# Reordering the opening of a hybrid convolution and sparse-attention layer: input rows first, small rotation angles, modulation in three parts, three projection tiles by channel tile

## What is computed

```python
mod = jax.nn.silu(c) @ w_ada + b_ada
shift, scale, gate = jnp.split(mod, 3, axis=-1)
h = rmsnorm(x, norm_in) * (1.0 + scale[:, None, :]) + shift[:, None, :]
proj = h @ w_in
(cb, cc, cu, cz, aq, ak, av, az, iq, ik, iw) = jnp.split(proj, cuts, axis=-1)
...
q = rope_partial(aq.reshape(Bsz, L, N_HEADS, HEAD_DIM), positions)
k = rope_partial(ak.reshape(Bsz, L, N_HEADS, HEAD_DIM), positions)
q_idx = rope_partial(iq.reshape(Bsz, L, N_IDX_HEADS, IDX_DIM), positions)
k_idx = rope_partial(ik[:, :, None, :], positions)[:, :, 0, :]
```

## Time and profile before

| | before |
|---|---|
| median of 3 runs | 732.51 us (732.18 to 734.01) |
| profiled execution, of which span | 737.07 us, 735.3 us |
| PE busy | 669.7 us, 91% of the span |
| PE weight loads busy | 552.7 us, 75% |
| DVE, ACT, POOL busy | 492.1, 364.9, 235.4 us |
| chain that ended last, by engine | PE 79%, DVE 8%, ACT 5%, issue 5%, DMA 2% |
| mean granted TensorE clock | 0.981 |

### The profile page before, as it was taken

How to read it: one execution, slowest core, us unless ns; L and a number is a source line. 1 busy time by engine, 2 the same in 40 slices (tenths; PEclk the granted TensorE clock), 3 DMA queues, 4 the chain that set the end, 5 groups by cost and what they waited for, 6 DMA issues and landing times.

```text
span 735.3 us, 8771 instructions
## 1 busy us (share of the span) xinstructions
PE 669.7 (91%) x3170; PEld 552.7 (75%) x3170; DVE 492.1 (67%) x737; ACT 364.9 (50%) x550; POOL 235.4 (32%) x113
## 2 busy tenths in 40 slices
PE   0489999899999999999999989998999988979996
PEld 0478988678888888888888877886777666758885
DVE  4786815677888899998079550014898988485734
ACT  1484435555563143452444434535787787783212
POOL 0003324432224152757766488420011110030000
PEclk9999999999999999999999999998999999989998
DMA  8902287353222110111100462075744340301531
GB/s 343 412 26 86 63 212 141 114 171 113 90 86 87 57 56 32 57 36 50 58 29 29 137 196 69 1 171 163 239 115 116 87 115 9 107 29 58 172 115 57
DMA packets 22661, 79.14 MB, mean 108 GB/s; under 512 B 3738, under 2 KB 4058, under 8 KB 21596
## 3 DMA queue, kind: packets, MB, share of 16 engines
q1 hardware_dynamic: 22620, 78.60, 35.2%
HBM read 61.77 MB, written 13.41 MB: 102 GB/s over the span
## 4 chain that ended last, share of the span: by engine, by line
PE 79%; DVE 8%; ACT 5%; issue 5%; DMA 2%; SPq 0%; ACTq 0%; DVEq 0%
PE ps L631 17%; PE ps L632 17%; PE ps L633 17%; PE ps L810 4%; PE ps L812 4%; PE ps L811 4%; PE ps L748 3%; DMA wa<-in_w_ada 2%; PE ps L689 2%; PE ps L690 2%; PE ps L670 2%; PE ps L671 2%; DVE phL L1384 2%; DVE acc L1178 1%; PE ps L761 1%
## 5 line engine op out<-in xcount | busy, mean ns | idle before, releaser
L631 PE MATMUL ps<-hH,wH 128*128 128x512 f32 (+1 forms) x592 | 230.3, 389 | 3.8 <-ACT wH L865 2.3
L632 PE MATMUL ps<-hL,wH 128*128 128x512 f32 (+1 forms) x592 | 228.3, 386 | 0.0
L633 PE MATMUL ps<-hH,wL 128*128 128x512 f32 (+1 forms) x592 | 228.1, 385 | 0.0
L1533 POOL TENSOR_TENSOR wL<-raw,wH 128x1024 fp32r<-128x1024 f32 x37 | 94.4, 2552 | 186.5 <-ACT wH L865 186.5
L631 PEld LDWEIGHTS ps<-hH,wH 128*128 128x128 f32 x592 | 111.9, 189 | 25.1 <-issue 3.0
L633 PEld LDWEIGHTS ps<-hH,wL 128*128 128x128 f32 x592 | 111.9, 189 | 21.5
L632 PEld LDWEIGHTS ps<-hL,wH 128*128 128x128 f32 x592 | 112.1, 189 | 19.2
L1376 DVE CUSTOM_DVE_ANT_0 ps<-ps,bias 128x128 f32<-128x128 f32 (+3 forms) x64 | 48.7, 761 | 45.6 <-PE ps L671 43.7
L1384 DVE TENSOR_TENSOR phL<-ps,phH 128x512 fp32r<-128x512 f32 (+1 forms) x96 | 52.7, 555 | 22.6 <-ACT phH L1040 18.5
L1020 ACT ACTIVATE relu<-ps,wabs 128x384 f32<-128x384 f32 (+5 forms) x48 | 40.1, 849 | 43.6 <-PE ps L690 17.5
L1270 DVE SCALAR_TENSOR_TENSOR score<-relu,wsgn,score 128x384 f32<-128x384 f32 (+5 forms) x42 | 49.7, 1183 | 17.2 <-ACT relu L1020 14.5
(11 more groups left out here) (206 smaller groups left out, 1102.9 us busy)
## 6 DMA issues: line engine op xcount, KB each, us to landing
raw<-in_w_units SPq DMA_DIRECT2D x36, 512.0 KB, 3.3
wa<-in_w_ada SPq DMA_DIRECT2D x8, 1024.0 KB, 8.8
ks<-qk_halves SPq DMA_DIRECT2D x32, 256.0 KB, 5.5
xin<-in_x SPq DMA_DIRECT2D x8, 512.0 KB, 12.5
gw<-in_w_ada SPq DMA_DIRECT2D x8, 512.0 KB, 4.4
qs<-qk_halves SPq DMA_DIRECT2D x16, 256.0 KB, 4.0
wo<-in_w_out SPq DMA_DIRECT2D x8, 512.0 KB, 9.3
xe<-in_x SPq DMA_DIRECT2D x8, 512.0 KB, 4.1
```

The costliest lines, as they stand in the source:

```text
L631: pe.matmul(out, wH[:, n % 2, kt, :], hH[:, kt, cols], start=(kt == 0), stop=False)
L632: pe.matmul(out, wH[:, n % 2, kt, :], hL[:, kt, cols], start=False, stop=False)
L633: mm = pe.matmul(out, wL[:, n % 2, kt, :], hH[:, kt, cols], start=False, stop=(kt == KT - 1))
L1533: g.tensor_tensor(wL[:, n % 2, :, :], raw[:, n % NRAW, :, :], wH[:, n % 2, :, :].bitcast(F32), ALU.subtract).then_inc(s_wL, 1)
```

## The change

- **Order of loads.** The positions (as 8 rows of 128), `w_ik` and x come first, `w_ada` after them.
- **Angles.** DVE works on 128x64 angles, 8 frequencies by 8 token tiles: PE transposes the positions, eight products make the angles, ACT takes sine and cosine, DVE widens each to 128x1024 (`wide`), PE transposes them in 16 tiles, and ACT copies them to `tabS` and `tabC`.
- **Modulation in parts.** The columns of `w_ada` are summed for channel tiles 0 to 3, 4 and 5, 6 and 7 (`PARTS`), each with its own `acc`, products and `shift` and `amp`. The first part is 8 DMAs of 512 KB in rows of 2 KB, the others 8 DMAs of 256 KB each in rows of 1 KB. The second part's buffers lie on those of the first, so SP waits for the first sum (`s_acc` of 8) before it issues them.
- **x.** The transposed channel tiles 2 to 7 are copied to `xT` by ACT without scale and shift (`STAGED`), and 0 and 1 stay in PSUM. ACT does all eight scalings and all eight roundings; DVE's three are gone.
- **Three units by channel tile.** Units 0, 1 and 2 run interleaved (`FIRST_STEPS`), with the products of modulation parts 2 and 3 among them. The weights have 4 slots at first; DVE makes `wL` of units 1 and 2. The transposes of `iw` move behind unit 3.

```diff
-NRAW = 2
+NFIRST = 3
+NSLOT = 4
-        ("iq", 0): [("iwt", 0)],
+        ("iq", 2): [("iwt", 0)],
-X_GROUPS = ((0, 4), (4, 6), (6, 7), (7, 8))
+X_GROUPS = ((0, 4), (4, 6), (6, 8))
+PARTS = ((0, 4), (4, 6), (6, 8))
+STAGED = (2, 3, 4, 5, 6, 7)
+X_TURNS = ((2, 2, 0), (3, 4, 0), (4, 6, 0), (5, 0, 0), (6, 2, 1), (1, 4, 2), (7, 6, 3), (0, 0, 4))
+FIRST_STEPS = ([(0, 0), (0, 1), (1, 0), (1, 1), (0, 2), (1, 2), (2, 0), (2, 1), (2, 2), (3, 0), "mod", (3, 1), (3, 2)]
+               + [(4, 0), (4, 1), (4, 2), (5, 0), "mod", (5, 1), (5, 2)]
+               + [(6, 0), (6, 1), (7, 0), (7, 1), (6, 2), (7, 2)])
...
+            sp.dma_start(posi[:], a["positions"].rearrange("o (b p) -> (o b) p", p=P)).then_inc(s_pos, 16)
+            load(0)
             for t in range(NB):
                 sp.dma_start(xin[:, t, :], a["x"][0, P * t:P * t + P, :]).then_inc(s_x[t], 16)
+            def load_part(g):
+                lo_k, hi_k = PARTS[g]
+                each = KT // len(wa[g])
+                for i, dst in enumerate(wa[g]):
+                    if g == 1 and i == 0:
+                        sp.wait_ge(s_acc, KT)
+                    for k in range(each):
+                        sp.dma_start(dst[:, k, :, :], w_cols[:, each * i + k, :, P * lo_k:P * hi_k]).then_inc(s_wa[g][i], 16)
+            load_part(0)
             load(1)
+            load(2)
+            load_part(1)
+            load_part(2)
+            load(3)
+            sp.dma_start(pairs[:], a["pairs"]).then_inc(s_pairs, 16)
+            for n in range(NSLOT, NSLOT + 2):
+                load(n)
...
+            pe.wait_ge(s_tab, 1)
+            modulation(0, 2)
+            pe.wait_ge(s_tab, 2)
+            part = 1
+            for at_step in FIRST_STEPS:
+                if at_step == "mod":
+                    if part > 1:
+                        pe.wait_ge(s_amp, part)
+                    modulation(part, 7)
+                    part += 1
+                else:
+                    first_unit(*at_step)
```

More of the change, by code:

```diff
@@ L433, in wait_low, with raw_count, wait_wl @@
                 waits.wait_ge(s_splP, m + 1 - NT)
[L435 to L438 removed]
+        def raw_count(n):
+            return 1 if n < NSLOT else (n - NSLOT) // 2 + 2
+        def wait_wl(waits, n):
+            if n in (1, 2):
+                waits.wait_ge(s_wLd, n)
             else:
[L440 removed]
+                waits.wait_ge(s_wL, max(1, n - 1))
         block = ctx.enter_context(nc.Block())
@@ new lines, in _, with table @@
+            for kt, bank, staged in X_TURNS[4:]:
+                pe.wait_ge(s_xt, staged)
+                for t in range(NB):
+                    mm = turn_x(kt, bank, t)
+                mm.then_inc(s_xtp, 1)
+            def table(src, bank):
+                for b in range(NB):
+                    mm = pe.transpose(two(bank)[:, P * b:P * b + P], src[:, b, :, :].rearrange("p r f -> p (r f)"), identF[:])
+                mm.then_inc(s_tabp, 1)
+            pe.wait_ge(s_wide, 1)
+            pe.wait_ge(s_xt, 5)
@@ new lines, in first_unit @@
+            def first_unit(kt, n):
+                pe.wait_ge(s_hH, kt + 1)
+                w = (S - IQ0) // 2 if UNITS[n][0] == "iq" else HALF
+                if kt == 0:
+                    pe.wait_ge(s_wH, n + 1)
+                for half in range(2):
+                    out = ps[:, 2 * slot(n) + half, 0:w]
+                    cols = slice(S - w * (2 - half), S - w * (1 - half))
+                    pe.matmul(out, wH[slot(n)][:, kt, :], hH[:, kt, cols], start=(kt == 0), stop=False)
+                    if kt == 0 and half == 0:
+                        wait_wl(pe, n)
+                    pe.matmul(out, wL[slot(n)][:, kt, :], hH[:, kt, cols], start=False, stop=False)
+                    if half == 0:
+                        pe.wait_ge(s_hL, kt + 1)
+                    mm = pe.matmul(out, wH[slot(n)][:, kt, :], hL[:, kt, cols], start=False, stop=(kt == KT - 1))
+                if kt == KT - 1:
+                    mm.then_inc(s_unit, 1)
@@ new lines, in _ @@
+            factors(0, 2)
+            first_low(1)
+            ada_sum(1, 0)
+            low_h(0)
+            first_low(2)
+            ada_sum(1, 1)
+            low_h(1)
+            ada_sum(1, 2)
+            low_h(2)
+            ada_sum(1, 3)
+            low_h(3)
+            ada_sum(2, 0)
+            factors(1, 7)
+            ada_sum(2, 1)
+            low_h(4)
+            ada_sum(2, 2)
+            low_h(5)
+            ada_sum(2, 3)
+            factors(2, 7)
+            low_h(6)
```

324 lines of the change are left out of this document (178 added, 146 removed).

## The result

The changed kernel took 728.86 us, the median of 8 runs (725.82 to 730.38), beside 733.06 us (732.18 to 736.91) for 8 runs of the kernel before: a ratio of 0.9932, 95% interval 0.9908 to 0.9956, so about 5.0 us less (3.2 to 6.7). The ratio is that of the means; the medians alone differ by 4.2 us. The forecast was 725.0 us, in a range of 722.5 to 731.0, and faster with a chance of 0.78. Its profiled execution took 727.11 us, where the forecast for a profiled one was 729.6. In the later comparisons one execution of each kernel took far longer (863.57 us before, 964.55 us after, at granted clocks of 0.76 and 0.66), and the ratios leave these out.

A forecast was written before the change was run, and what follows sets the result against it. PE bounds the kernel from 56.5 us, so the opening's saving counts as what it moves unit 5 forward: 98.2 to 90.7, 7.5 us. On the median, 732.5 - 7.5 = 725.0 us, range 722.5 to 731.0.

The forecast's parts named there:

- Loads, angles, normalisation: Opening: squares from 9.4 us, last x group ready at 20.9 and done at 22.5, part 1's sum ending at 32.0.
- The rival of slow rows: `w_ada` loads: rows of 2 and 1 KB stream badly, part 1 takes 24.2 us, total 735.7; chance 0.10.
- The 42 us: Part 1's 16 loads of 256 KB: estimate by the skill's fit if they did not overlap, kernel some 30 us slower.
- the fast pace: PE in the opening: 0.12 us per record, so part 1's products take 1.9 us, to 34.0, factors at 34.7.
- the slow pace: Part 1's products on PE: 0.21 to 0.22 us per record instead of 0.12, which would add 1.5 us.
- The 16 x 0.12: Part 1's one-column products on PE: 16 at 0.12 us each, 1.9 us in all.
- Channel tiles: Units 0 to 2: `hH` 0 at 37.0, `hL` 1 at 42.0, 1.4 us lost at each of tiles 4 and 6.
- The rival that the clock falls in these stalls: Channel tiles 4 and 6: one or two falls of PE's clock, total 726.7 to 728.4 us; chance 0.20.
- Unit 5: DVE chain of 14.0 us, weights at 90.6, PE waits 1 us, start about 90.7 instead of 98.2: 7.5 earlier.
- The step that failed: Behind unit 6's weights: every step hangs on PE's own evacuations as before, and 3.8 us of `relu` waits stay.
- 98 to 110 us, 90% busy for 173 GB/s: Old trace's DMA window, used as the rate for slow `w_ada` rows: part 1 in 24.2 us, to 40.4.
- Its own sign of being wrong: Behind the opening: the forecast is wrong if a later wait grows by what the opening gains.

The follow-up runs named there:

- fillers: Changed kernel plus 14 and 22 transposes that nobody reads, ahead of and behind the products of part 1: 726.69 us, ratio 0.9911 to the kernel before.
- repeats of after: Changed kernel run twice more, unedited: first repeat 728.06 us, ratio 0.9909 to the kernel before; traced executions 728.69 and 726.71 us.
- repeats of before: Kernel before run twice more, unedited, each as one execution: 731.92 and 734.81 us.
- later scores: Changed kernel with the first group of index scores moved from step 4 of its unit to step 8: 725.58 us, ratio 0.9885 to the kernel before.
- all three edits: Changed kernel with filler transposes, index scores after 8 steps, and POOL's third split after DVE turned `ik`: 721.65 us, ratio 0.9834 to the kernel before.
- `w_ada` first: Changed kernel with part 1 of `w_ada` loaded and summed ahead of x: 737.67 us, ratio 1.0046 to the kernel before.
- units one by one: Changed kernel with units 0, 1 and 2 one after the other instead of interleaved: 736.68 us, ratio 1.0042 to the kernel before.
- later split: Changed kernel with POOL's third split waiting until DVE has turned `ik`: 725.88 us, ratio 0.9883 to the kernel before.
- parts together: Changed kernel with all modulation parts summed and multiplied before the first projection product: 741.76 us, ratio 1.0111 to the kernel before.

## Why the prediction held, point by point

**Direction and mechanism were right.** PE's dense row of products bounds the kernel, and what the opening saves counts at unit 5. Undoing the interleaving, the parts or the order of the loads each gives back the whole gain and ends 3 to 8 us behind the kernel before.

**Loads, angles, normalisation.** Squares at 8.22 (forecast 9.4), the last x group normalised at 20.5 (22.5), the sum of part 1 at 31.0 (32.0). The forecast for accumulations was 1.25 each; they took 1.38 (9.63/7), and the earlier start paid for that. The rival of slow rows was wrong: 390 and 354 GB/s, and no wait for `w_ada`. The 42 us worked out from the fit of the Trainium skill (DMA: Bandwidth & Descriptors, Anatomy of one DMA), for 16 loads that do not overlap, did not come. The page gives its fit for DMAs that GpSimd issues, and these are SP's; here SP issued the 16 from 30.98 to 40.04 us and they landed 5.9 us behind their issue in the median, so they did overlap.

**The transposes and products of part 1: half wrong.** The transposes took the fast pace, as forecast, and `tabS` was out at 29.3 instead of 32.1. That opened the hole: the sum ended only at 31.0, PE idled for 2.04 us, and the products took 3.25 instead of 1.9. The step "it has transposed densely since 19 us, so I take the fast pace" looked at the work before the products, not at the gap between. I had priced the slow pace at 1.5; the measured difference is 1.3 (3.25 against 1.93 with fillers), and 0.9 in both repeats (2.86 and 2.85). The 16 x 0.12 counts records; the products are 8. The factors came at 34.8 (34.7) all the same, since all in front was a microsecond early.

**Channel tiles.** `hH` 0 at 37.1 (37.0), `hL` 1 at 42.1 (42.0), 1.2 us lost at each of tiles 4 and 6 (1.4), the products of parts 2 and 3 at 0.95 (1.0), unit 3 at 72.7 (72.2) without a gap. The rival that the clock falls in these stalls was wrong: the windows from 42 to 116 us read 1.00, and the only mark of the stalls is the single products right behind a wait, 0.50 us instead of 0.40.

**Unit 5.** Chain of DVE 14.07 us (14.0), weights ready at 91.24 (90.6), a gap of 1.06 (1), start at 91.34 (90.7). Over three traces each the gain is 6.5 us instead of 7.5: 0.8 of it from the later start in the new kernel (91.5 for 90.7; in the first trace DVE begins `ik` at 72.96 for the 72.3 of the forecast), 0.2 from the old one's mean (98.0 for 98.2).

**The step that failed** is "from there every step hangs on PE's own evacuations as before; the 3.8 us of `relu` waits stay". What stands there is a queue of transfers. SP's last issue of `iqs` and a window of the kernel after:

```profile
105.74 1.87 SPq L540 DMA_DIRECT2D iqs<-hlL  x3
...
110.00:116.00 6.00, 6.00 (x28) 4.95 (x28) 0.00 (x0) 2.55 (x3) 2.54 (x4) 1.00 1.04 205
```

The same two of the kernel before:

```profile
110.16 1.87 SPq L502 DMA_DIRECT2D iqs<-hlL  x3
...
110.00:116.00 6.00, 6.00 (x28) 4.95 (x28) 3.50 (x3) 3.47 (x4) 2.40 (x1) 1.00 1.05 181
```

In both, the DMA engines are busy all the time and move half of what they can (205 and 181 GB/s beside 390 at 20 to 25 us). The last issues end at 107.6 and 112.0, and the piece lands about 12 us behind, at 119.44 in the kernel after. The queue runs empty in the windows of one microsecond that follow, first in the kernel before, then in the kernel after:

```profile
123.00:124.00 1.00, 1.00 (x6) 0.88 (x5) 0.65 (x1) 0.98 (x2) 0.00 (x0) 1.00 0.06 16
```

```profile
119.00:120.00 1.00, 0.56 (x3) 0.59 (x4) 1.00 (x1) 0.00 (x0) 1.00 (x1) 1.00 0.04 16
```

So the transfers came some 4 us earlier. PE, though, reaches the first score at 116.78, before at 123.42, 6.6 earlier, and waits 2.66 us. In the kernel before it came less than 1 us behind the queue's end, and in one repeat it waited 1.4 us for it. The working in the prediction had the seed of it: it put unit 3's evacuation 5.4 us earlier (86.3 for 91.70; it was 4.7) and unit 5's start 7.5, and the stores and loads of the turned units follow the evacuation. I read the earlier trace rows at 98 to 110 us, 90% busy for 173 GB/s, as a price for the loads of `w_ada` and not as the queue that it is.

**Why the step cost next to nothing.** The `relu` waits did not stay, and what they lost is about what the DMA wait gained. The table has each trace from unit 5 to the last index score, in us; PE busy is that of the stretch.

| | stretch | waits of PE, the longest | granted clock, ten us at that wait | PE busy |
|---|---|---|---|---|
| before | 123.8 | 3.8, 3.1 | 0.83 | 120.0 |
| repeats of before | 122.2, 124.9 | 3.6, 1.5 and 3.7, 2.9 | 1.00 and 0.66 | 118.6 and 121.2 |
| after | 123.5 | 3.4, 2.7 | 0.83 | 120.1 |
| repeats of after | 124.3, 124.4 | 4.1, 3.4 and 4.0, 3.3 | 0.83 and 0.83 | 120.2 and 120.3 |
| fillers | 122.6 | 4.1, 3.4 | 1.00 | 118.5 |
| later scores | 121.7 | 3.1, 1.6 | 1.00 | 118.6 |
| all three edits | 122.1 | 3.8, 2.3 | 1.00 | 118.3 |

The waits sum to 3.6 to 3.8 us before and 3.4 to 4.1 after. Moving the scores takes the DMA wait away and brings 3.1 us of `relu` back, which bears the exchange out. That the total came out as forecast is luck, since the prediction had no DMA wait in it and kept all of the other. Its own sign of being wrong, a later wait that grows by what the opening gains, came in part: 2.7 of the 6.5 us.

The rest is the clock. Behind the long wait it falls in both kernels, in two traces of three before and in all three after. The kernel before, then the kernel after:

```profile
130.00:140.00 10.00, 7.80 (x29) 6.62 (x30) 6.29 (x10) 4.56 (x8) 1.25 (x1) 0.83 0.39 129
```

```profile
120.00:130.00 10.00, 10.00 (x41) 8.46 (x40) 7.77 (x7) 3.52 (x7) 4.46 (x2) 0.83 0.37 114
```

PE is busy for 118.3 to 118.6 us in the stretch where the clock reads 1.00 and for 120.0 to 121.2 where it fell, so by these rows one fall costs 1.4 to 2.9 us, as much as the differences that the single edits were meant to show. With fillers the wait was as long as in a repeat of after (3.4 us) and the clock did not fall, for which no run here shows a reason. The later scores owe the larger part of their 121.7 us to the clock, for their waits are 0.7 shorter than the mean of after.

**The size.** The forecast saving was 7.5 us. Measured are 5.0 (3.2 to 6.7) and, in the repeat, 6.7 (4.3 to 9.2, from the ratio and 733.85 us of before). On the marks 1.0 of it is missing at unit 5 and 0.5 more by the last index score, which is less than the traces of one kernel differ there (122.2 to 124.9). The rest of the 3.9 us between 725.0 and 728.86 is not a step of the change that I can name: it is within the interval.

## What to carry to other kernels

Put the forecast's shift of each feeder of the bound engine (evacuation, store, reload) beside the shift of the engine itself: where the feeder moves less, a new wait will stand. Then look at what stands behind it, for the new wait can take the place of an old one, as 2.7 us of DMA wait did here for 3.1 of `relu`, and only the sum is the price. A window in which the DMA engines are full at half their rate is a queue with a landing time of its own, even if nobody waits for it yet. Take two or three traces of each kernel before you build on a microsecond: a fall of the clock behind a wait comes in one execution and not in the next. Small edits that take the same slack from one another can show nothing singly and 0.8% together (0.9834 beside 0.9909), so the last run should hold them all.

## What the runs showed of the hardware

- The granted clock falls in some of PE's waits, and the same wait does not always bring it down. The 16 records of part 1's products took 1.92 us behind a wait of 0.33 us (`w_ada` first), 2.24 behind 1.50 (units one by one), 2.52 behind 1.65 (later split), 2.86 and 2.85 behind 1.82, 3.25 behind 2.04, 3.44 behind 2.14 (parts together), but 1.92 again behind 2.44 us (later scores). Without fillers the first projection products ran at half pace in each of these traces (to 41.6 us in the kernel after), with fillers in none. The gaps of 0.5 to 1.1 us at 55 to 91 us did not lower the clock.
- A single wait of 2.7 to 3.6 us for a DMA or `relu` between 116 and 135 us was followed by a fall of the granted clock in eight traces (before and one repeat, after and both repeats, the units one by one, `w_ada` first, the later split) and by none in two (fillers, 3.4 us; parts together, 3.0 us). In the four traces where the longest wait was 2.3 us or less it stayed at 1.00.
- A DVE `tensor_tensor` with both inputs in SBUF that starts beside a running POOL operation ends 1.07 and 1.08 us after POOL's (79.97 against 78.90, and 81.47 against 80.39), so it is held until POOL is done and then takes most of its own time. One that is already running keeps its 1.22, and in the kernel before it is POOL's that grows: 3.15 instead of 2.40 us, started at 78.22 beside a DVE operation of 77.93 to 79.14. The Trainium skill (GPSIMD Engine Reference, 1. Specifications) names contention of the two engines for DVE instructions with two SBUF inputs; the traces agree, and the price here is 2.2 us for DVE.
- Loads of 256 KB in 1 KB rows, issued back to back, stream at 354 GB/s beside other work (36 to 42 us).
- The landing of x scatters by 0.7 us from run to run, and moves unit 5 with it (91.99 against 91.34).
